# Shared PSUM banks for the modulation rows, and x's transpositions ahead of them, in a two-block transformer kernel

## The reference

```
m = silu(cvec) @ w_mod + b_mod                 # for c and for c_ctx: six vectors of 1024
sh1, sc1, gt1, sh2, sc2, gt2 = split(m, 6)
hl = rmsnorm(x, g_mix) * (1 + sc1) + sh1       # 256 latent tokens
hc = rmsnorm(ctx, g_mix) * (1 + csc1) + csh1   # 256 context tokens, with c_ctx's vectors
k, v from both (hl, hc) @ w_kv;  q from hl @ w_q;  u, vv from gelu(hl @ w_gm)
mix = concat(attention(q, k, v), u * (w_s @ vv + b_s))
x = x + gt1 * (mix @ w_out)
h = rmsnorm(x, g_ffn) * (1 + sc2) + sh2
x = x + gt2 * experts(h)        # 16 experts, 32 tokens each, chosen by softmax(h @ w_router)
```

## Time and profile before

| what | value |
|---|---|
| median of three runs | 1453.25 us (1453.12 to 1453.58) |
| the profiled execution's own time | 1443.64 us |
| its span, first to last instruction | 1441.8 us |
| PE busy | 1003.8 us (70%) |
| DVE, ACT, POOL busy | 333.1, 248.8, 111.3 us |
| mean granted clock of TensorE | 0.847 |
| DMA in slices 7 to 30 of 40 (about 216 to 1081 us) | nearly all tenths at 9, some 428 GB/s |
| read from HBM | 481.21 MB |

### The profile page before, as it was taken

How to read it: one execution, slowest core, us unless ns; L and a number is a source line. 1 busy time by engine, 2 the same in 40 slices (tenths; PEclk the granted TensorE clock), 3 DMA queues, 4 the chain that set the end, 5 groups by cost and what they waited for, 6 DMA issues and landing times.

```text
span 1441.8 us, 14665 instructions
## 1 busy us (share of the span) xinstructions
PE 1003.8 (70%) x6403; PEld 496.4 (34%) x6403; DVE 333.1 (23%) x801; ACT 248.8 (17%) x508; POOL 111.3 (8%) x89
## 2 busy tenths in 40 slices
PE   4899876666675656656566556656665688889976
PEld 3675832112121111111111111111111687679865
DVE  4657520000001000000000000000000648445661
ACT  3535210000000000000000000000000645443451
POOL 1210000000020000000000000000000462300032
PEclk9999977888778878887877787787878799989998
DMA  9696669999999999999999999999998241334401
GB/s 401 262 393 240 252 261 428 428 427 429 428 426 427 428 427 429 427 427 428 428 428 428 429 427 429 428 428 428 427 428 369 95 175 60 117 117 176 168 8 44
DMA packets 34992, 483.21 MB, mean 335 GB/s; under 512 B 3886, under 2 KB 3888, under 8 KB 5744
## 3 DMA queue, kind: packets, MB, share of 16 engines
q1 hardware_dynamic: 34240, 479.92, 79.6%
q0 software_dynamic: 400, 1.31, 0.3%
q10 hardware_dynamic: 288, 1.05, 0.2%
HBM read 481.21 MB, written 1.05 MB: 334 GB/s over the span
## 4 chain that ended last, share of the span: by engine, by line
DMA 54%; PE 32%; DVE 6%; ACT 5%; issue 1%; POOL 0%; DVEq 0%; SPq 0%; POOLq 0%; ACTq 0%
DMA ring<-in_t_w 53%; PE PS L465 8%; PE PS L477 6%; PE PS L952 6%; PE PS L999 2%; ACT S L591 2%; PE PS L455 1%; PE PS L732 1%; PE PS L752 1%; PE PS L963 1%; DMA ring<-in_t_mod 1%; PE PS L655 1%; PE PS L938 1%; DVE S L572 1%; ACT RR L430 1%
## 5 line engine op out<-in xcount | busy, mean ns | idle before, releaser
L952 PE MATMUL PS<-ring,S 128*32 128x512 f32 x2048 | 320.7, 760 | 210.1 <-DMA ring<-in_t_w 207.6
L999 PE MATMUL PS<-ring,S 128*32 128x512 f32 x1024 | 174.1, 813 | 117.8 <-DMA ring<-in_t_w 110.4
L952 PEld LDWEIGHTS PS<-ring,S 128*32 128x32 f32 x2048 | 63.2, 126 | 455.5 <-DMA ring<-in_t_w 326.9
L465 PE MATMUL PS<-RR,SR 128*128 128x512 f32 (+4 forms) x376 | 109.4, 396 | 15.6 <-DVE RR L633 6.8
L999 PEld LDWEIGHTS PS<-ring,S 128*32 128x32 f32 x1024 | 33.3, 129 | 239.9 <-DMA ring<-in_t_w 163.8
L477 PE MATMUL PS<-SR,RR 128*128 128x256 f32 x608 | 93.6, 283 | 2.0 <-DVE RR L1468 2.0
L485 ACT ACTIVATE S<-PS 128x512 f32<-128x512 f32 (+3 forms) x58 | 32.5, 566 | 359.1 <-PE PS L455 318.4
L430 ACT ACTIVATE RR<-ring 128x1024 fp32r<-128x1024 f32 (+3 forms) x95 | 89.6, 1005 | 7.3 <-DMA ring<-in_t_o_g 4.3
L1816 ACT ACTIVATE S<-PS 128x512 f32<-128x512 f32 x16 | 9.6, 597 | 455.3 <-PE PS L952 455.3
L477 PEld LDWEIGHTS PS<-SR,RR 128*128 128x128 f32 x608 | 84.8, 190 | 2.9 <-DVE RR L1468 2.4
L465 PEld LDWEIGHTS PS<-RR,SR 128*128 128x128 f32 x376 | 72.6, 199 | 31.7 <-DVE RR L633 7.5
(11 more groups left out here) (279 smaller groups left out, 937.6 us busy)
## 6 DMA issues: line engine op xcount, KB each, us to landing
ring<-in_t_w SPq DMA_DIRECT2D x192, 2048.0 KB, 31.3
ring<-in_t_mod SPq DMA_DIRECT2D x12, 2048.0 KB, 12.8
ring<-in_t_out SPq DMA_DIRECT2D x6, 2048.0 KB, 7.8
ring<-in_t_e_g SPq DMA_DIRECT2D x2, 2048.0 KB, 7.7
ring<-in_t_o_q SPq DMA_DIRECT2D x2, 2048.0 KB, 7.8
ring<-in_t_o_k SPq DMA_DIRECT2D x2, 2048.0 KB, 7.8
ring<-in_t_o_v SPq DMA_DIRECT2D x2, 2048.0 KB, 8.4
ring<-in_t_o_g SPq DMA_DIRECT2D x2, 2048.0 KB, 8.3
```

Source lines behind the costliest of these rows:

```text
L465: m = pe.e.matmul(PS[:, b, 0:width], l_, r_, start=(k == 0 and n == 0), stop=(k == k8 - 1 and n == 2))
L952: m = pe.e.matmul(PS[32 * j:32 * j + 32, b, :], XE[:, 2 * k + kk, 32 * e_:32 * e_ + 32], place[name, e_, k][:, kk, 512 * j:512 * j + 512], ...
L999: m = pe.e.matmul(PS[q:q + 32, b, :], HT[e_ % 2][:, 128 * s + 32 * j:128 * s + 32 * j + 32], place["w2", e_, j][:, s, 512 * dh:512 * dh + ...
```

## The change

Two or six modulation units now share one PSUM bank. `cvec` is twice as wide, and unit j of a group multiplies with a window of it that is moved by 2j columns, so that its rows land 2j rows lower in the bank, with zeros added to the other rows. One copy to `bm` and one `mod_cols` with 16 output columns serve the group. The groups are s0 (first halves of sc1 and sh1), s1 (second halves), a (gt1, sc2, sh2, six units, in bank 7, held) and g (gt2, two units, held until its second unit). The places of the matmuls among keys and values, of the copies and of the splits of the output weights in the turns change too, x's transpositions come before the first `mod_part`, the squares come before the silus, and POOL's tables wait for the normalised x and ctx. The router's row sh2 @ w_router is made as one row and spread to 128 partitions by another matmul after the loop. One more `out_part(n2, True)` is in the turns. Of the two `beside` shown, the first is TensorE's and the second ScalarE's.

```diff
+MODG = {"s0": [("sc1", 0), ("sh1", 0)], "s1": [("sc1", 1), ("sh1", 1)], "a": MODS[4:10], "g": MODS[10:]}
+ROW_OF = {"s0": 0, "s1": 1, "a": 0, "g": 1}
...
-    bm = sb("bm", 3, 512)
+    bm = sb("bm", 2, 512)
-    cvec = sb("cvec", 8, 32)
+    cvec = sb("cvec", 8, 64)
...
+        def mod_part(g, j):
+            name, n = MODG[g][j], len(MODG[g])
+            key, w = ("mod", g), place[name]
+            if j == 0:
+                banks.take(key, ALL6 if g != "a" else (OB[1],), hold=True)
+                pe.wait_ge(banks.was[key], ("cv", 0), ("cv", 1))
+            b = banks.of[key]
+            pe.wait_ge(("load", name))
             for k in range(8):
                 q = k % 4
-                m = pe.e.matmul(PS[32 * q:32 * q + 32, b, :], cvec[:, k, :], w[:, k, :], start=k < 4, stop=k >= 4)
+                m = pe.e.matmul(PS[32 * q:32 * q + 32, b, :], cvec[:, k, 32 - 2 * j:64 - 2 * j], w[:, k, :],
+                                start=j == 0 and k < 4, stop=j == n - 1 and k >= 4)
...
-        mod_part("sc1", 0)
         pe.wait_ge(*[("xn", i) for i in range(4)])
         for k in range(8):
             transposes(pe, ("raw", k), ALL6, [(XN if i < 2 else XC)[:, i % 2, 128 * k:128 * k + 128] for i in range(4)])
-        mod_cols("sc1", 0)
-        mod_part("sh1", 0)
-        mod_cols("sh1", 0)
+        mod_part("s0", 0)
+        mod_part("s0", 1)
+        mod_cols("s0")
+        mod_part("s1", 0)
         for i in range(4):
             banks.take(("kv", i), ALL6, hold=True)
             pe.wait_ge(banks.was["kv", i])
-        kv_part(range(4))
-        mod_part("sc1", 1)
-        mod_cols("sc1", 1)
-        mod_part("sh1", 1)
-        mod_cols("sh1", 1)
-        kv_part(range(4, 8))
+        kv_part(range(2))
+        mod_part("s1", 1)
+        kv_part((2,))
+        mod_cols("s1")
+        kv_part(range(3, 8))
...
         def beside():
-            mod_part(*A1_MODS[0])
-            yield
-            mod_part(*A1_MODS[1])
-            mod_cols(*A1_MODS[0])
-            yield
-            mod_part(*A1_MODS[2])
-            mod_cols(*A1_MODS[1])
-            yield
-            mod_cols(*A1_MODS[2])
+            for n in range(3):
+                mod_part("a", n)
+                yield
             yield
             for i in range(2):
                 mixed(i)
                 yield
-            for n in range(3, 8):
-                mod_part(*A1_MODS[n])
+            for n in range(3, 6):
+                mod_part("a", n)
                 yield
-                if n < 6:
-                    mod_cols(*A1_MODS[n])
-                elif n == 6:
-                    shifted()
                 yield
-            for n2 in range(2):
+            mod_cols("a")
+            yield
+            mod_part("g", 0)
+            yield
+            mod_part("g", 1)
+            yield
+            shifted()
+            out_part(0, True)
+            yield
+            for n2 in (1, 2):
                 out_part(n2, True)
                 yield
...
-        for n2 in range(2, 4):
-            out_part(n2, True)
+        out_part(3, True)
+        shift_spread()
...
         def beside():
-            for n in range(3):
-                mod_row(*A1_MODS[n])
+            for _ in range(5):
                 yield
-            for _ in range(2):
+            for i in range(2):
+                mixture_high(i)
                 yield
-            mixture_high(0)
             yield
-            mixture_high(1)
-            for n, c in ((3, 4), (4, 6), (5, 0), (6, 2)):
-                mod_row(*A1_MODS[n])
-                yield
+            for c in (4, 6, 0):
                 hi_piece(act, ("out1", 0), c)
                 yield
-            mod_row(*A1_MODS[7])
+            mod_row("a", ("col", "s0"))
+            yield
+            hi_piece(act, ("out1", 0), 2)
             yield
             hi_piece(act, ("out1", 1), 4)
             yield
+            mod_row("g", ("col", "s1"))
             hi_piece(act, ("out1", 1), 6)
             yield
...
-        outputs_low(1)
         rest(side)
+        outputs_low(1)
+        lo_piece(dve, ("out1", 1), 2)
         dve.stage("router")
-        for n2 in range(2, 4):
+        for n2 in range(1, 4):
             x1_add(n2, True)
...
-        pool.wait_ge("squares act", "squares dve")
+        pool.wait_ge("squares act", "squares dve", ("load", "consts"))
         rstd(pool, rs1, ss1, "rs1")
+        pool.wait_ge(("xn", 3))
```

More of the change, by code:

```diff
@@ L723, in pe_program, with mod_cols @@
         pe.wait_ge(("load", "consts"))
-        def mod_part(name, h):
-            key, w = ("mod", name, h), place[name, h]
-            b = banks.take(key, ALL6)
-            pe.wait_ge(banks.was[key], ("cv", 0), ("cv", 1), ("load", (name, h)))
+        def mod_part(g, j):
[6 more added lines that the diff above has]
+            pe.wait_ge(("load", name))
             for k in range(8):
                 q = k % 4
-                m = pe.e.matmul(PS[32 * q:32 * q + 32, b, :], cvec[:, k, :], w[:, k, :], start=k < 4, stop=k >= 4)
-            m.then_inc(*pe.mark(used((name, h)), key))
-        def mod_cols(name, h):
-            key = ("col", name, h)
+                m = pe.e.matmul(PS[32 * q:32 * q + 32, b, :], cvec[:, k, 32 - 2 * j:64 - 2 * j], w[:, k, :],
+                                start=j == 0 and k < 4, stop=j == n - 1 and k >= 4)
+            m.then_inc(*pe.mark(used(name), *([key] if j == n - 1 else [])))
+            if j == n - 1:
+                banks.release(key)
+        def mod_cols(g):
+            key = ("col", g)
             b = banks.take(key, ALL6)
-            pe.wait_ge(banks.was[key], out_of(("mod", name, h)))
-            row = bm[:, MODS.index((name, h)) % 3, :]
+            pe.wait_ge(banks.was[key], out_of(("mod", g)))
             for s in range(4):
-                m = pe.e.matmul(PS[:, b, 2 * s:2 * s + 2], row[:, 128 * s:128 * s + 128], quarters[:, 0:2], start=True,
+                m = pe.e.matmul(PS[:, b, 16 * s:16 * s + 16], bm[:, ROW_OF[g], 128 * s:128 * s + 128], quarters, start=True,
                                 stop=True)
@@ L912, in pe_program @@
         for h in range(2):
[L913 to L915 removed]
+            pe.wait_ge(out_of(("mod", "g")))
+            m = pe.e.matmul(PS[64 * h:64 * h + 64, b, :], quarters[:, 2 * h:2 * h + 1].to_broadcast([P, 64]),
+                            bm[:, ROW_OF["g"], :], start=True, stop=True)
         m.then_inc(*pe.mark("g2"))
@@ L1322, in beside @@
             yield
-            yield
-            x1_add(0, True)
-            lo_piece(dve, ("out1", 1), 4)
-            yield
-            x1_add(1, True)
-            lo_piece(dve, ("out1", 1), 6)
-            yield
-            for c in (0, 2):
+            for c in (4, 6):
                 lo_piece(dve, ("out1", 1), c)
                 yield
+            yield
+            dve.wait_ge("shift row")
+            copy_out(dve, "shift row", bbs[0:1, :], PS[0:1, banks.of["shift row"], 0:16])
+            lo_piece(dve, ("out1", 1), 0)
+            x1_add(0, True)
+            yield
         def outputs_low(i):
@@ L1665, in act_program @@
         act.stage("mix")
-        act.wait_ge(("load", "consts"), "cvec zero")
-        for r in range(2):
-            act.e.activation(cvec[:, :, r], RT[:, 8 * r:8 * r + 8], ACT.Silu).then_inc(*act.mark(("cv", r)))
         act.wait_ge(("load", "x"))
@@ L1673, in act_program, with mod_row @@
             *act.mark("squares act"))
-        def mod_row(name, h):
-            n = MODS.index((name, h))
-            act.wait_ge(("mod", name, h), ("col", *MODS[n - 3]) if n >= 3 else None)
-            copy_out(act, ("mod", name, h), bm[:, n % 3, :], PS[:, banks.of["mod", name, h], :])
-        mod_row("sc1", 0)
+        act.wait_ge(("load", "consts"), "cvec zero")
+        for r in range(2):
+            act.e.activation(cvec[:, :, 32 + r], RT[:, 8 * r:8 * r + 8], ACT.Silu).then_inc(*act.mark(("cv", r)))
+        def mod_row(g, before=None):
+            act.wait_ge(("mod", g), before)
+            copy_out(act, ("mod", g), bm[:, ROW_OF[g], :], PS[:, banks.of["mod", g], :])
         for k in range(1, 8, 2):
```

94 lines of the change are left out of this document (51 added, 43 removed).

## The result

The changed kernel takes **1436.4 us** (median of 1436.08, 1436.32, 1436.48 and 1440.43) beside 1453.18 for the kernel before (median of 1453.12, 1453.25, 1453.58 and 1445.05): ratio 0.9902 (0.9881 to 0.9923), so 16.8 us faster in the medians and 14 by the ratio. The ratios in this text are not quotients of the two medians (here 0.9885) and lie nearer to those of the means (here 0.9904). The sign is as forecast, but the forecast of 1442.9 and its range, 1439.5 to 1446.8, lie above the time. The profiled execution took 1436.08 us, 7.6 less than that of before (1443.64).

A forecast was written before the change was run, and what follows sets the result against it. Expert-weight transfers (53% of the span) start with the first expert matmul, so earlier work moves the end one for one: 10.7 gained less 0.3 lost in attention is 10.4, 1453.25 to 1442.9 us, range 1439.5 to 1446.8.

The forecast's parts named there:

- Start, keys and values: Up to the queries: 10.7 us gained, 1.7 start, 5.4 between the fours, 3.2 clock, 0.4 bank.
- waits of 0.7 to 1.6 us leave the clock at 1.00: Keys and values: the new PE waits were taken to keep full clock, with 3.2 us of gain from the clock.
- The rival of a clock that falls again among the slices: Keys and values: the clock falls again, 2.7 us lost, 1445.6 us; chance 0.18.
- Attention: First scores to the attention's part of the output product, 62.9 us before: a loss of 0.3, bounds minus 4 to plus 3.
- The waits ahead of the values: Attention, scores 3 to 5: PE waits 2.9 us for ScalarE's copy of the probabilities, behind a split of 1.06.
- the loss that was laid out for the queues: Attention, PE, DVE and ACT queues: gains 2.6 and 0.1, losses 1.1 and 1.9, in sum a loss of 0.3 us.
- the slower rival: Attention: the clock falls behind the new waits; 30 us from n = 3 on at half clock gives 1473; chance 0.03.
- The router: After attention, ahead of the experts: same chain; one more `x1_add` on DVE fits in PE's 2.8 us.
- One for one to the end: First expert matmul, 191.41 us before: what moves it moves the end equally, as the expert stream's length is fixed by bytes.
- The sum against the median: Whole kernel: 10.4 us subtracted from the median 1453.25 gives 1442.9; the 9.6 above the profiled execution taken as another rate.
- A sum against the profile's own time: Whole kernel, profiled execution: 10.4 us earlier, from 1443.64 to 1433.2.
- the 6 or more that PE alone would have given: Attention: 6 us or more gained if PE alone set the time, from removed columns' products, copies and waits.

The follow-up runs named there:

- the order experiment: Changed kernel with ScalarE's copy of the transposed probabilities ahead of its split of the output weights from n = 4 on: 1435.23 us (0.9909).
- the late start: Changed kernel with ScalarE's square of the context repeated 8 more times at the start: mean of 12 executions 1447.1 us, median 1447.15.
- The three delays: Changed kernel with DVE's router scan repeated 14 or 7 more times, or ScalarE's square at the start 8 more: means 1449.0, 1443.4 and 1447.1 us.

## Why the prediction was right or wrong

**Start, keys and values: right in size.** The gain of 10.7 at the queries was 10.24 (56.73 to 46.49), and over the two profiles of before and the four of the changed kernel 11.0 in the mean. One step was not sound: that waits of 0.7 to 1.6 us leave the clock at 1.00. In two of the four profiles it fell ahead of the third unit, behind idle times of 0.88 and 0.97 us, and cost 1.5 to 1.6 us of PE, of which about 1.2 reached the first key matmul. The rival of a clock that falls again among the slices didn't come.

**Attention: right in size, by luck.** A loss of 0.3 was forecast, and 0.1 measured (62.9 to 63.0). The waits ahead of the values came at their places, and the order experiment shows that ScalarE's queue makes them. But the forecast had full clock throughout. With full clock the same queues took 61.3 us, a gain of some 1.5; the changed kernel lost it again because one burst of values ran at half clock, 3.59 us instead of 1.95. So the loss that was laid out for the queues was 1.8 us too large, and a loss that was not in the sum made up for it. It is the mechanism of the slower rival in small, at 1.6 us and not 30: the windows show 0.93 from 110 to 130 us. The Trainium skill (TensorE: Matmul & The Clock Gate, section "A second HAM failure mode: psum-queue depth-cycling") tells of a kernel whose clock swings because PE is idle for short times between groups of matmuls that cycle through PSUM banks; the trace agrees for this one burst, 1.6 us, and only the profile of the late start shows it at a second burst. The router took 36.0 us to the first expert instead of 35.7.

**One for one to the end: right, to about 2 us.** From the first profile of before to that of the changed kernel, 9.9 us at the first expert became 7.6 at the end, with 1.2 lost in the experts and 1.2 behind them. The three delays came through as 12.0 for 10.6, 6.4 for 5.8 and 10.2 for 10.2.

**The sum against the median: this step failed.** The text took the 9.6 us between the profiled execution (1443.64) and the median (1453.25) "as the same stream at another rate" and subtracted 10.4 from the median. The runs show another thing. The profile is an execution of the shorter group, with 310 us behind the second block's first matmul; the three runs shown were, by their times, of the longer group, and from its upper end (the group's mean is 1451.8, the pooled median 1450.9). The changed kernel's median lies in its shorter group. The difference of the two groups, 6 us, is time in the second block in the profiles that show it, where the change touches nothing, and the range had no term for it. From group to group the gain is near the forecast 10.4: 1445.7 to 1435.9 is 9.8, and 1451.8 to 1441.0 is 10.8. Between the pooled means, 1449.8 and 1436.9, it is 12.9: 9.8, and 67% less 21% of 6.15 us, 2.8, for the smaller share of long executions, and 0.2 for the rest. The pooled medians make 14.6 of it, and the first comparison, three of four long against one of four, 16.8. A sum against the profile's own time gave 1433.2; it took 1436.08. The miss of 2.9 has its terms in the table: 0.5 at the first expert, 1.2 in the experts, 1.2 in the rest.

**Open.** Why 67% of the executions of before are long and 21% of the changed kernel's. The moment alone was tried by the delays and doesn't settle it. What makes one execution take the one pattern and the next the other, in the same program, is open too, and so is why the clock falls ahead of the third unit or behind the wait for values in some executions and not in others: the lengths of the waits don't sort them.

## What to carry to other kernels

Before a gain is taken from a median, see which of the kernel's executions the profile is: here one program has two lengths 6 us apart, and a change of 10 us read as 10, 13, 15 or 17 by what was compared. Where one wait for a stream starts the rest, give the time of that one instruction, before and after; it was within 1 us of the forecast in all four profiles. A stretch that comes out as forecast can still hide two errors: compare the bursts in it with the same bursts elsewhere. And work taken out of one engine brings little where the queues beside it now do theirs in the wrong order (1.5 us here of the 6 or more that PE alone would have given): put the copy that the next matmul waits for ahead of the one that nobody waits for yet.

## What the hardware showed

- The first transposes ran at less than full pace in every profile with this start: 32 of them took 6.55 us from 14.55 on (5.16 to 6.55 in twelve profiles), and 5.35 from 23.35 on with the late start, where 3.78 is the least with a `mod_part` ahead of them. The windows show a granted clock of 1.00 there (14 to 21 us), as they do where the first `mod_part` of the kernel before takes 3.64 us and later ones 1.92: at the program's start the column doesn't show the pace. The `mod_part` right behind took 1.82 for each unit, full pace.
- The length of a wait alone doesn't tell whether the granted clock falls. Ahead of the third unit it fell with 0.88 and 0.97 us of idle time and stayed with 1.35 and 1.46, in profiles of the same kernel; behind the wait of 2.65 us for the values it fell in eight of ten profiles.
- The second block took the granted clock in two patterns, in which the same 16 records of L1077 took 2.05 or 3.47 us, and the stretch to the queries 108.5 or 113.9 (1124.12 to 1232.64, 1123.76 to 1237.69), in one and the same program. A third, with 312.5 us for the rest, came once.
- An unread f32 matmul of 128x128 by 128x512 took about 0.88 us, one of a modulation unit, on 32 columns of the array, 0.24 (1.93 for the 8 of a unit, in 16 records).
- DVE's products took 1.42 and 1.41 a pair, where they took 1.49 and 1.49 before with POOL's tables running beside them. Whether the tables are the reason was not tried.
